# Two recurrent layers and an attention-and-experts block on one core: both norms between blocks taken one row tile at a time

## The reference

```python
for l in range(2):
    h = rmsnorm(x, g[0]); y = mixer(h)            # even: 10 column blocks in, odd: 6
    x = x + rmsnorm(y, g[1])
    h = rmsnorm(x, g[2])
    x = x + rmsnorm(sq_relu_mlp(h, w1, w2), g[3])
mod = silu(c) @ w_ada + b_ada                      # 6 vectors: shift, scale, gate, twice
h = modulate(rms_norm(x, g_norm1), sh1, sc1)       # then attention and a convolution
x = x + ga1 * (merged @ w_o)
h2 = modulate(rms_norm(x, g_norm2), sh2, sc2)
x = x + ga2 * moe(h2)                              # 32 experts of three 1024x512 weights
```

## Time and profile before

| | before |
|---|---|
| time, median of 3 runs (lowest to highest) | 1455.51 us (1454.21 to 1455.75) |
| the profiled execution: its time, its span | 1457.32 us, 1454.0 us |
| TensorE busy | 1261.0 us, 87% of the span |
| VectorE, ScalarE, POOL busy | 645.5, 242.6, 85.5 us |
| mean granted TensorE clock | 0.935 of full speed |
| chain that ended last | TensorE 70%, DMA 21%, VectorE 5%, ScalarE 2% |

### The profile page before, as it was taken

The page is one execution under the profiler, slowest core; times in us unless marked ns, Lnnn a source line. Parts: engine busy times, 40 slices in busy tenths (PEclk is TensorE's granted clock), DMA queues, the critical chain, the costliest instruction groups (busy, mean ns, idle before and its releaser), DMA issues.

```text
span 1454.0 us, 15281 instructions
## 1 busy us (share of the span) xinstructions
PE 1261.0 (87%) x6465; PEld 795.1 (55%) x6465; DVE 645.5 (44%) x834; ACT 242.6 (17%) x483; POOL 85.5 (6%) x81
## 2 busy tenths in 40 slices
PE   8999999999999999999999999999863665636747
PEld 5855847995455774998445888555321222212212
DVE  6478425566965762556886574415100100101001
ACT  2321302330010331232002233113000000000000
POOL 0046201000010001000001100000000000000000
PEclk9999999999999999999999999999987878868778
DMA  9533334448962324345993433486999999999997
GB/s 352 181 118 116 116 130 160 174 174 294 350 223 101 132 80 179 118 175 189 349 370 133 173 116 118 173 361 275 394 428 426 428 429 426 429 427 428 426 427 271
DMA packets 94390, 376.95 MB, mean 259 GB/s; under 512 B 7248, under 2 KB 7920, under 8 KB 82416
## 3 DMA queue, kind: packets, MB, share of 16 engines
q1 hardware_dynamic: 93728, 373.84, 66.2%
q0 software_dynamic: 576, 2.10, 0.4%
q10 hardware_dynamic: 16, 0.00, 0.0%
HBM read 374.88 MB, written 1.05 MB: 259 GB/s over the span
## 4 chain that ended last, share of the span: by engine, by line
PE 70%; DMA 21%; DVE 5%; ACT 2%; issue 1%; POOL 0%; DVEq 0%; SPq 0%; ACTq 0%; POOLq 0%
PE PS L995 13%; PE PS L951 12%; PE PS L736 12%; PE PS L776 9%; DMA weights<-in_w 8%; PE PS L719 7%; DMA arena<-in_w 6%; PE PS L1218 5%; DMA proj_rows<-in_w 4%; PE PS L1256 3%; DMA normalised<-in_w 2%; PE PS L983 2%; PE PS L679 2%; PE PS L919 1%; PE PS L859 1%
## 5 line engine op out<-in xcount | busy, mean ns | idle before, releaser
L1218 PE MATMUL PS<-weights,x_rows 128*32 128x512 f32 x368 | 133.1, 728 | 43.1 <-DMA proj_rows<-in_w 21.6
L995 PE MATMUL PS<-weights,arena 128*128 128x512 f32 x384 | 167.4, 592 | 0.0
L736 PE MATMUL PS<-weights,normalised 128*128 128x256 f32 x720 | 160.5, 380 | 3.3 <-DVE weights L1775 2.6
L736 PEld LDWEIGHTS PS<-weights,normalised 128*128 128x128 f32 x720 | 135.8, 190 | 25.3 <-issue 6.1
L2330 DVE TENSOR_TENSOR x_rows<-x_rows,PS 128x512 f32<-128x512 f32 x8 | 8.4, 1046 | 286.7 <-PE PS L1218 286.7
L1218 PE MATMUL PS<-arena,x_rows 128*32 128x512 f32 x256 | 97.6, 724 | 42.4 <-DMA weights<-in_w 29.9
L776 PE MATMUL PS<-weights,arena 128*128 128x512 f32 x288 | 125.4, 594 | 2.7 <-ACT arena L1626 1.4
L995 PEld LDWEIGHTS PS<-weights,arena 128*128 128x128 f32 x384 | 72.8, 190 | 90.9 <-issue 90.9
L1218 PE MATMUL PS<-proj_rows,x_rows 128*32 128x512 f32 x240 | 79.2, 709 | 42.9 <-DMA normalised<-in_w 22.5
L719 PE MATMUL PS<-weights,normalised 128*128 128x512 f32 x256 | 111.9, 595 | 1.0 <-ACT normalised L1418 0.8
L951 PE MATMUL PS<-normalised,weights 128*128 128x128 f32 x896 | 106.9, 275 | 0.0
(11 more groups left out here) (350 smaller groups left out, 1769.1 us busy)
## 6 DMA issues: line engine op xcount, KB each, us to landing
weights<-in_mlp_w SPq DMA_DIRECT2D x32, 2048.0 KB, 8.8
weights<-in_w SPq DMA_DIRECT2D x32, 2048.0 KB, 34.7
arena<-in_w SPq DMA_DIRECT2D x24, 2048.0 KB, 34.8
...
```

The costliest lines, as they stand in the source:

```text
L736: last = mm(at, lhs[:, k, :], rhs[:, k, :], start=(first and k == 0), stop=(k == 3), skip_group_check=not first)
L995: last = mm(PS[:, bank, :], lhs[:, k0 + i, rows], rhs[:, i, :], start=(g == 0 and i == 0), stop=(g == NGRP - 1 and i == 1))
L1218: last = mm(PS[CAP * x:CAP * (x + 1), 4 + kind, :], XG[:, k, CAP * x:CAP * (x + 1)], w[:, k, :], start=(k == 0), stop=(k == KT - 1), tile_ ...
```

## The change

Both norms of a seam are done for tile 0 first.

- `seam_powers` replaces `y_powers` and `norm_powers` at the seams: POOL takes y of tile 0, x of tile 0, y of tile 1, x of tile 1.
- `norm` is split into `scaled_rows(tt)` and `transposed(tt)`, `transpose_stream` into `tile_transposes(n, tt)`. VectorE's `mixer_seam` and `mlp_seam` bring tile 0 up to its transposed halves before tile 1's y is added.
- The first up block runs tile by tile (128 moving columns instead of 256), with the second tile's transposes ahead of its column group 3; `proj_block` has them ahead of its k = 6 (at the program's start, k = 2) inside tile 0.
- The `keep_warm` products at the four seams are gone.
- The modulation is split: TensorE's one-column products no longer wait for the rows of y, the row sums go to banks 2 and 3, and both stand before the transposes of tile 0. In the MLP seam y times gain goes to a buffer of its own (`GY`) and no longer waits for the square of y. VectorE adds the gate's row sums after tile 1's x.
- At the start, VectorE's three operations on the lower bounds come between the two tiles.

Line numbers of the changed kernel are a little larger than those before: L1744 and L1740 are the product with the gain (L1729), L1748 the addition to x (L1733), L1710 the scaling (L1700), L1724 the transposed half (L1710), L678 a transpose, L992 the up block (L983), L722 the projection (L719), L766 and L774 the modulation.

The diff, cut to its core:

```diff
+        GY = PRF[:, 8 * K1:10 * K1].rearrange("p (t n) -> p t n", t=TT)
...
-            def y_powers(r):
-                mean_power(2, None, "y_sq", 3 * r + 1)
-                mean_power(3, 5, "y_sq", 3 * r + 3)
+            def seam_powers(n):
+                mean_power(2, None, "y_sq", 3 * n - 2)
+                mean_power(0, None, "x_sq", 3 * n + 1)
+                mean_power(3, 5, "y_sq", 3 * n)
+                mean_power(1, 4, "x_sq", 3 * n + 3)
...
+            def tile_transposes(n, tt):
+                pe.wait_ge(sem("xn_ready"), 2 * n + tt + 1)
+                for half in range(2):
+                    quad(4 + 2 * tt + half, [XN[:, tt, (4 * half + j) * P:(4 * half + j + 1) * P] for j in range(4)])\
+                        .then_inc(sem("xT_ready"), 1)
             def transpose_stream(n, warm=0):
-                for q in range(4):
-                    tt, half = q // 2, q % 2
-                    if q == 2:
-                        keep_warm(7, warm)
-                    if half == 0:
-                        pe.wait_ge(sem("xn_ready"), 2 * n + tt + 1)
-                    quad(4 + q, [XN[:, tt, (4 * half + j) * P:(4 * half + j + 1) * P] for j in range(4)])\
-                        .then_inc(sem("xT_ready"), 1)
+                tile_transposes(n, 0)
+                keep_warm(7, warm)
+                tile_transposes(n, 1)
...
                     for k in range(KT):
+                        if norm is not None and tt == 0 and k == (6 if norm else 2):
+                            tile_transposes(norm, 1)
                         last = mm(PS[:, 2 * (n % 2) + tt, :], HT[:, k, tt * P:(tt + 1) * P], wn(s)[:, k, :],
                                   start=(k == 0), stop=(k == KT - 1))
...
-            def modulation(l):
+            def column_modulation(l):
                 pe.wait_ge(sem("ada_free"), ADA * ADA_PARTS * (l + 1))
-                pe.wait_ge(sem("y_rows"), 3 * l + 1)
                 for j in range(4):
                     for n in range(4):
-                        mm(PS[:, 7, 4 * j + n:4 * j + n + 1], AC[:, j, n * P:(n + 1) * P], ONE[:, 0:1],
-                           start=True, stop=True)
+                        last = mm(PS[:, 7, 4 * j + n:4 * j + n + 1], AC[:, j, n * P:(n + 1) * P], ONE[:, 0:1],
+                                  start=True, stop=True)
+                last.then_inc(sem("mod_raw"), 1)
+            def row_modulation(l):
+                pe.wait_ge(sem("y_rows"), 3 * l + 2)
                 for j in range(2):
-                    last = mm(PS[:, j, :], ONE, AC[:, 4 + j, :], start=True, stop=True)
+                    last = mm(PS[:, 2 + j, :], ONE, AC[:, 4 + j, :], start=True, stop=True)
                 last.then_inc(sem("mod_raw"), 1)
...
-            transpose_stream(0)
+            tile_transposes(0, 0)
...
-                keep_warm(7, 5)
-                transpose_stream(norm)
+                tile_transposes(norm, 0)
                 s = slot_of(base)
                 pe.wait_ge(sem(f"slot{s}_full"), fulls(base))
-                for j in range(4):
-                    for k in range(KT):
-                        if j == 0 and k % 4 == 0:
-                            pe.wait_ge(sem("hT_ready"), 4 * norm + 3 + k // 4)
-                        last = mm(PS[:, 4 + j // 2, (j % 2) * T:(j % 2 + 1) * T],
-                                  wn(s)[:, k, j * P:(j + 1) * P], HT[:, k, :],
-                                  start=(k == 0), stop=(k == KT - 1))
-                    if j == 1:
-                        last.then_inc(sem("hid_raw"), 1)
+                for tt in range(TT):
+                    for j in range(4):
+                        if tt == 0 and j == 3:
+                            tile_transposes(norm, 1)
+                        for k in range(KT):
+                            if j == 0 and k % 4 == 0:
+                                pe.wait_ge(sem("hT_ready"), 4 * norm + 2 * tt + k // 4 + 1)
+                            at = (j % 2) * T + tt * P
+                            last = mm(PS[:, 4 + j // 2, at:at + P], wn(s)[:, k, j * P:(j + 1) * P],
+                                      HT[:, k, tt * P:(tt + 1) * P], start=(tt == 0 and j % 2 == 0 and k == 0),
+                                      stop=(k == KT - 1), skip_group_check=True)
+                        if tt and j == 1:
+                            last.then_inc(sem("hid_raw"), 1)
...
-                modulation(l)
+                column_modulation(l)
+                row_modulation(l)
+                tile_transposes(norm + 1, 0)
             mlp(0, B_MLP0, 1)
-            pe.wait_ge(sem("y_rows"), 3)
-            keep_warm(6, 2)
-            transpose_stream(2)
...
+            def mixer_square(n):
+                act.wait_ge(sem("y_done"), n)
                 a(XN[:, 0, :].rearrange("p (a b) -> p a b", a=2), PS[:, 0:2, :], ACT.Square,
                   scale=D ** -0.5, accum_out=ST[:, 2:3]).then_inc(sem("y_sq"), 1)
+                act.wait_ge(sem("y_done"), n + 1)
+                a(XN[:, 1, LEFT], PS[:, 2, :], ACT.Square, scale=D ** -0.5, accum_out=ST[:, 3:4])\
+                    .then_inc(sem("y_sq"), 1)
+                stream_square(n, 0)
+                act.wait_ge(sem("block_used"), Y_BLOCKS[n // 2] + 1)
+                a(XN[:, 1, RIGHT], PS[:, 3, :], ACT.Square, scale=D ** -0.5, accum_out=ST[:, 5:6])\
+                    .then_inc(sem("y_sq"), 1)
+                stream_square(n, 1)
+                stream_square(n, 2)
...
+                row_square(1, 0, slice(0, D), 2)
+                row_square(2, 1, RIGHT, 5)
+                stream_square(2 * l + 2, 0)
+                row_square(3, 1, LEFT, 3)
+                if l:
+                    high_half(4, 0)
+                stream_square(2 * l + 2, 1)
+                stream_square(2 * l + 2, 2)
+                if l:
+                    high_half(4, 1)
...
+            def scaled(r, tt, at, count):
+                if r % 2:
+                    link(v.tensor_tensor(GY[:, tt, at], XN[:, tt, at], GB[:, at], ALU.mult))
+                else:
                     dve.wait_ge(sem("y_sq"), 3 * r + count)
+                    y = PS[:, 2 * tt:2 * tt + 2, :].rearrange("p a b -> p (a b)")[:, at]
                     link(v.tensor_tensor(XN[:, tt, at], y, GB[:, at], ALU.mult))
+            def added(r, tt, at, count):
+                tell(v.scalar_tensor_tensor(X[:, tt, at], (GY if r % 2 else XN)[:, tt, at], ST[:, 2 + tt:3 + tt],
+                                            X[:, tt, at], ALU.mult, ALU.add), "x_new", 3 * r + count)
+            def second_added(r):
+                rstd()
+                added(r, 1, LEFT, 2)
+                added(r, 1, RIGHT, 3)
+                dve.sem_inc(sem("res_done"), 1)
+            def mixer_seam(r, gain):
                 dve.wait_ge(sem("gain_in"), 16 * (r + 1))
+                scaled(r, 0, slice(0, D), 1)
                 rstd()
+                added(r, 0, slice(0, D), 1)
+                scaled(r, 1, LEFT, 2)
+                scaled_rows(0)
+                transposed(0, gain)
+                scaled(r, 1, RIGHT, 3)
+                second_added(r)
+                scaled_rows(1)
+                transposed(1, gain)
...
-            norm(GC[:, R_G:R_G + 8])
-            row_halves(B_EV_IN)
+            scaled_rows(0)
+            transposed(0, GC[:, R_G:R_G + 8])
+            scaled_rows(1)
             dve.wait_ge(sem("lb_in"), 16)
             link(v.tensor_tensor(BO, LB[:, 0, :], LB[:, 1, :], ALU.max))
             link(v.tensor_tensor(BO, BO, LB[:, 2, :], ALU.max))
             tell(v.tensor_tensor(LB, LB, midb(BO, 3), ALU.subtract), "lb_shifted", 1)
+            transposed(1, GC[:, R_G:R_G + 8])
+            row_halves(B_EV_IN)
...
+            def mlp_seam(l, base):
+                p0, r = 6 * l, 2 * l + 1
                 dve.wait_ge(sem("y_p1"), l + 1)
                 dve.wait_ge(sem("y_part"), p0 + 2)
+                v.tensor_tensor(XN[:, 0, LEFT], YA1, PS[:, 1, :], ALU.add)
                 dve.wait_ge(sem("y_part"), p0 + 3)
                 link(v.tensor_tensor(YA1, YA1, PS[:, 2, :], ALU.add))
                 dve.wait_ge(sem("y_part"), p0 + 4)
+                link(v.tensor_tensor(XN[:, 0, RIGHT], YA1, PS[:, 3, :], ALU.add))
                 dve.wait_ge(sem("y_part"), p0 + 5)
+                tell(v.tensor_tensor(XN[:, 0, RIGHT], XN[:, 0, RIGHT], PS[:, 4, :], ALU.add), "y_rows", 3 * l + 1)
+                dve.wait_ge(sem("gain_in"), 16 * (r + 1))
+                scaled(r, 0, slice(0, D), 1)
                 dve.wait_ge(sem("y_part"), p0 + 6)
                 link(v.tensor_tensor(YA1, YA1, PS[:, 5, :], ALU.add))
+                tell(v.tensor_tensor(XN[:, 1, RIGHT], YA1, PS[:, 3, :], ALU.add), "y_rows", 3 * l + 2)
+                rstd()
+                added(r, 0, slice(0, D), 1)
                 dve.wait_ge(sem("block_used"), base + MLP_B)
+                tell(v.tensor_tensor(XN[:, 1, LEFT], YA1, PS[:, 6, :], ALU.add), "y_rows", 3 * l + 3)
```

(17 more changed lines are left out.)

145 lines of the change are left out of this document (48 added, 97 removed).

## The result

| | before | changed |
|---|---|---|
| median (lowest to highest), 6 runs each | 1455.45 us (1454.16 to 1455.81) | 1440.02 us (1436.07 to 1441.62) |
| ratio, 95% interval | | 0.9891 [0.9880, 0.9902] |
| profiled execution, its span | 1457.32, 1454.0 us | 1437.69, 1435.8 us |
| TensorE, VectorE, ScalarE, POOL busy | 1261.0, 645.5, 242.6, 85.5 us | 1240.9, 645.6, 242.5, 83.4 us |
| mean granted TensorE clock | 0.935 | 0.939 |

The forecast was 1443.0 in 1438 to 1450: the change is faster by 15.4 us, or 1.1%, and 12.5 were forecast. The profiled execution gained 19.6 us, and the other runs of the same kernel lie up to 3.9 us above it. TensorE does 20.1 us less of listed work: four sets of idle products are gone, and some half-speed time.

A forecast was written before the change was run, and what follows sets the result against it. TensorE, busy 87% of the span, was taken to bound the kernel up to the expert stage; 9.5 (mixer seams) + 4.0 (MLP seams) - 1.0 (start) = 12.5 us off 1455.5 gives 1443.0 us, range 1438 to 1450.

The forecast's parts named there:

- Mixer seams, 4.75 each: At the two mixer seams, tile 0's up-block products cover tile 1's norm: 4.75 us gained each, 9.5 together.
- The 0.4 for the narrower products: Up block as 64 products of 128 columns instead of 32 of 256: 14.3 us against 13.89, 0.4 more per block.
- MLP seams, 2.0 each: At the two MLP seams the norm hides behind the modulation; with the clock falling, 2.0 us gained each, 4.0 together.
- rival 2: The clock does not fall at the MLP seams: 17.3 us gained in all, 1438.2 us; chance 0.10.
- The norm ready 4.5 us after the columns begin: At the MLP seams, tile 0 is ready for its transposes 4.5 us after the one-column products begin.
- The steps behind it: At the MLP seams, the first block starts 2.13 us after the first transpose, 2.78 at the second seam.
- Start, +1.0: At the program's start, waiting for first weights and moving tile 1's transposes inside costs 1.0 us, inside 0 to 2.5.
- VectorE behind at the next blocks: After the MLP seams, the next block's column sums end within 1 us of its start; VectorE's later idle time catches up.
- Rival 1: Without idle products the clock falls at mixer seams and block starts, 1.7 us per stretch: 1449 us; chance 0.12.
- Rival 3: The gain is lost later, to VectorE running behind or expert loads not moving: 1455 us at worst; chance 0.03.
- Rival 4: The split up block's 128 extra weight loads come into the open, 24.6 us instead of 0.8: 1466.8 us; chance 0.03.

The follow-up runs named there:

- kernel 5: Changed kernel with its MLP seams put back as before, so only mixer seams and start are changed: 1445.45 us, ratio 0.9942.
- kernel 9: Changed kernel with its mixer seams put back as before, so only MLP seams and start are changed: 1450.88 us, ratio 0.9977.
- kernels 1 and 10: The first is the changed kernel again, unaltered: 1443.17 us; the second is the changed kernel with the old program start: 1442.21 us.
- kernel 3: Changed kernel with one-column products made 128 columns wide and the row sums moved behind tile 0's transposes: 1437.07 us, ratio 0.9878.
- kernel 6: Changed kernel with both tiles transposed first and the up block back in 256-column products: 1453.34 us, ratio 0.9989.
- kernel 7: Kernel before the change with only its up block split into 128-column products, tile by tile: 1457.23 us, ratio 1.0017.

## Why the prediction was right

- **Mixer seams, 4.75 each: right**, 4.78 and 4.86 in the trace, 9.65 us for both with the start in kernel 5. Each intermediate time at the first seam (scaling, block, second transposes, end) came within 0.1 us. The 0.4 for the narrower products was 0.47.
- **MLP seams, 2.0 each: right in kind, and right in size partly by luck.** The step said that "I expect the clock to fall at both seams". It does not fall with certainty but by chance: the same seam of the same kernel took 23.02 us without a fall and 26.37 with one, 3.4 and 0.1 us less than before. The mean of the six traces is 23.45 and 24.42, that of the three with the old seams 25.98 and 26.89, so by them the term measured 2.5 + 2.5 = 5.0 instead of 4.0. In the profiled execution it was 7.85, near rival 2's 8.3. By the medians it was 3.3 in kernel 9 (1.9 to 4.7 by its interval), and the whole gain less kernel 5's 9.65 leaves 5.8 in the first measurement and 2.6 and 2.3 in kernels 1 and 10. So 4.0 lies inside what was measured, but as a mean over executions with and without a fall, not as the price of a certain one.
- **The norm ready 4.5 us after the columns begin: too early**, 5.06 in kernel 3. Most of it is POOL's pair, which I took with the 1.07 us of the mixer seam: here 1.51 us pass from the end of the square to VectorE's scaling, as the power takes longer:

```profile
426.86 0.98 POOL L597 TENSOR_TENSOR stats<-stats 128x1 f32<-128x1 f32 x1
```

At the mixer seam it took 0.57, and the kernel before already had 1.04 at this place (433.08). The norm stayed hidden only because the modulation takes 5.29. The steps behind it (2.13 and 2.78 to the block, measured 2.14 and 2.78) held.
- **Start, +1.0: oversized.** It was 0.56 in the first trace. The weights did decide, but over nine traces with the new start the second block begins anywhere in 1.5 us, and against the five with the old one the new start costs nothing that can be told.
- **VectorE behind at the next blocks: right.** The last column sum that the second weight block needs ended at 443.61 + 1.22 = 444.83, 1.0 us ahead of it at 445.81, and 0.5 us ahead at the second seam. TensorE did not wait.
- **Rival 1** (the clock falls at the mixer seams) did not occur in any trace of a kernel with the changed mixer seams intact, where TensorE waits 0.2 and 0.5 us; in kernel 6 the clock fell at both, during a wait of 5.8 us. **Rival 2** described the profiled execution (no fall), but not the kernel: the forecast and this rival are two outcomes of one program. **Rival 3** fell with the expert loads, 16.9 us earlier. The wait of 13.2 us in the earlier trace rows is that of a later expert load, after 978 us; the loads at 949.40 stand behind a load of out-projection weights that itself waited 13.3 us for L776. TensorE releases both, so the conclusion held. **Rival 4** fell with kernel 7.

The Trainium skill (TensorE: Matmul & The Clock Gate, Part 1) advises against long idle gaps between bursts of products, and I weighed it against the removal of the idle products, though the gaps left by it are short. Kernel 6 agrees with it for the gap of 5.77 us. At gaps of 0.2 and 0.5 us, without idle products, the clock stayed at 1.00 in eight traces.

The difference of 2.9 us between the gain forecast and the first one measured is no more than what two measurements of this kernel differ by (15.4 and 12.2 us around the 12.5 of the forecast). In the profiled execution, which gained 19.6, the sum missed 3.85 us at the MLP seams, where the clock did not fall, 0.4 at the start, 0.1 at the mixer seams, and the 1.6 us of the gather, which it did not contain.
